# Moving the first transposed operands of a blocked triangular inversion ahead, and waiting group by group

## The reference

```
L = where(tri_strict, einsum('bhnid,bhnjd->bhnij', k_beta, kc) * decay, 0.0)
A = L + eye(C)
rhs = concatenate([vc * bc[..., None], k_beta * exp(gc)[..., None]], axis=-1)
sol = triangular_solve(A, rhs, left_side=True, lower=True, unit_diagonal=True)
u, w = sol[..., :Dv], sol[..., Dv:]
```

## Time and profile before

| | us |
|---|---|
| median of 3 runs | 2391.99 (2386.74 to 2392.05) |
| profiled execution, its own time | 2380.26 |
| its span | 2378.5 |
| TensorE busy | 2283.2 (96%) |
| VectorE busy | 1521.1 (64%) |
| ScalarE busy | 1071.8 (45%) |
| GpSimd busy | 540.3 (23%) |

### The profile page before, as it was taken

One profiled execution on the slowest core, in us unless ns is written; L12 is line 12 of the kernel. 1 busy time (PEld: TensorE's weight loads), 2 busy tenths in 40 slices (PEclk: granted clock), 3 DMA queues, 4 the chain that ended last, 5 costly groups with the idle time before them and its releaser, 6 DMA issues.

```text
span 2378.5 us, 41225 instructions
## 1 busy us (share of the span) xinstructions
PE 2283.2 (96%) x17949; PEld 2190.6 (92%) x17949; DVE 1521.1 (64%) x1826; ACT 1071.8 (45%) x1354; POOL 540.3 (23%) x276
## 2 busy tenths in 40 slices
PE   7998999999999989999999999998999999998999
PEld 7997988899989989898999999878999999878999
DVE  6854676677769256666766655686555655686554
ACT  2653356443345433654344434545344434546433
POOL 0923304499527232046500000000000000000000
PEclk8997999999999979999999999999999999999999
DMA  9751034667657300446655555423555555423553
GB/s 286 247 190 36 1 125 142 213 232 247 213 166 254 130 18 1 159 157 208 205 183 188 175 180 186 150 90 116 186 185 188 175 180 187 150 89 125 182 191 124
DMA packets 332862, 384.22 MB, mean 162 GB/s; under 512 B 12551, under 2 KB 315402, under 8 KB 332554
## 3 DMA queue, kind: packets, MB, share of 16 engines
q1 hardware_dynamic: 332234, 381.42, 49.0%
q10 hardware_dynamic: 448, 0.16, 0.0%
HBM read 380.51 MB, written 1.05 MB: 160 GB/s over the span
## 4 chain that ended last, share of the span: by engine, by line
PE 79%; DVE 11%; ACT 6%; issue 2%; DMA 0%; SPq 0%; ACTq 0%; DVEq 0%
PE bank L697 16%; PE bank L698 15%; PE bank L699 15%; PE bank L920 5%; PE bank L921 5%; PE bank L922 5%; DVE weights_low L1310 4%; ACT weights_high L1985 3%; PE bank L1115 2%; PE bank L1134 2%; PE bank L971 1%; DVE arena L1412 1%; PE bank L711 1%; PE bank L1093 1%; PE bank L983 1%
## 5 line engine op out<-in xcount | busy, mean ns | idle before, releaser
L1310 DVE TENSOR_TENSOR weights_low<-ring,weights_high 128x2048 fp32r<-128x2048 f32 x302 | 743.1, 2461 | 458.0 <-ACT weights_high L1985 457.9
L697 PE MATMUL bank<-h_high,weights_high 128*128 128x256 f32 x3296 | 943.5, 286 | 23.4 <-DVE weights_low L1310 14.2
L698 PE MATMUL bank<-h_low,weights_high 128*128 128x256 f32 x3296 | 928.4, 282 | 0.0
L699 PE MATMUL bank<-h_high,weights_low 128*128 128x256 f32 x3296 | 927.9, 282 | 0.0
L1985 ACT ACTIVATE weights_high<-ring 128x2048 fp32r<-128x2048 f32 x302 | 578.1, 1914 | 705.7 <-PE bank L699 521.6
L697 PEld LDWEIGHTS bank<-h_high,weights_high 128*128 128x128 f32 x3296 | 623.0, 189 | 40.5 <-DVE weights_low L1310 22.3
L698 PEld LDWEIGHTS bank<-h_low,weights_high 128*128 128x128 f32 x3296 | 623.9, 189 | 3.0 <-issue 2.9
L699 PEld LDWEIGHTS bank<-h_high,weights_low 128*128 128x128 f32 x3296 | 623.9, 189 | 0.0
L920 PE MATMUL bank<-hidden_high,weights_high 128*128 128x256 f32 x1056 | 300.3, 284 | 1.3 <-DVE hidden_low L1551 0.8
L921 PE MATMUL bank<-hidden_low,weights_high 128*128 128x256 f32 x1056 | 299.7, 284 | 0.0
L922 PE MATMUL bank<-hidden_high,weights_low 128*128 128x256 f32 x1056 | 299.5, 284 | 0.0
(11 more groups left out here) (409 smaller groups left out, 3101.8 us busy)
## 6 DMA issues: line engine op xcount, KB each, us to landing
ring<-in_w_in SPq DMA_DIRECT2D x80, 1024.0 KB, 5.1
ring<-in_w_up SPq DMA_DIRECT2D x44, 1024.0 KB, 5.3
ring<-in_ffn_w_gate SPq DMA_DIRECT2D x44, 1024.0 KB, 5.2
ring<-in_ffn_w_up SPq DMA_DIRECT2D x44, 1024.0 KB, 5.2
ring<-in_ffn_w_down SPq DMA_DIRECT2D x44, 1024.0 KB, 4.9
side<-in_w_ada SPq DMA_DIRECT2D x42, 1024.0 KB, 7.6
ring<-in_w_down SPq DMA_DIRECT2D x22, 1024.0 KB, 5.0
ring<-in_w_dn_out SPq DMA_DIRECT2D x8, 1024.0 KB, 5.1
```

The source lines that it names most:

```text
L697: mm(o[:, m, :], a_, high[:, t, :], start=(t == 0), stop=False)
L698: mm(o[:, m, :], a_, low[:, t, :], start=False, stop=False)
L699: last = mm(o[:, m, :], b_, high[:, t, :], start=False, stop=(t == KT - 1))
L1310: v.tensor_tensor(low, wide(q), high.bitcast(F32), ALU.subtract).then_inc(chunk_split, 1)
```

## The change

Level 0 is taken out of VectorE's loop over levels and written out by two helpers: `first_turned(g)` makes YT of a group and counts a new semaphore `yt_first`; `first_level(g)` makes Y and counts `y_updated`. YT of groups 0 and 1 is made inside the preparation, after `exponents(2)` and `rows(1)`; then come, after the preparation, YT 2, Y 0, Y 1, YT 3, Y 2, Y 3. Level 0's transposes wait for three groups' preparation instead of four, level 1's products of group g for g + 3 (at most 4) updates instead of four. GpSimd's level 1 mask waits for `yt_first` of its group, and TensorE's second product of level 1 too.

```diff
@@ -1101,9 +1102,9 @@
                         if s == 0 and g < 2:
-                            pe.wait_ge(d_rows, 4 * l + 4)
+                            pe.wait_ge(d_rows, 4 * l + 3)
                         if s == 1:
-                            pe.wait_ge(y_updated, 4 * (LEVELS * l + 1))
+                            pe.wait_ge(y_updated, 4 * LEVELS * l + min(g + 3, 4))
@@ -1126,6 +1127,8 @@
                         pe.wait_ge(w_copied, wn + 1)
+                        if s == 1:
+                            pe.wait_ge(yt_first, 4 * l + g + 1)
@@ -1688,11 +1691,28 @@
+                def first_turned(g):
+                    dve.wait_ge(offdiag_ready, 4 * LEVELS * l + g + 1)
+                    v.tensor_tensor(YT[:, g, :, :], over(ident, 4), LO[:, g, :, :], ALU.subtract).then_inc(yt_first, 1)
+
+                def first_level(g):
+                    dve.wait_ge(winv_done, 4 * LEVELS * l + g + 1)
+                    v.tensor_tensor(Y[:, g, :, :], over(ident, 4), f4(B[g % 2][:, :]), ALU.subtract).then_inc(y_updated, 1)
+
                 for g in range(5):
                     if g < 4:
                         exponents(g)
                     if g >= 1:
                         rows(g - 1)
+                    if g == 2:
+                        first_turned(0)
+                        first_turned(1)
+                first_turned(2)
+                first_level(0)
+                first_level(1)
+                first_turned(3)
+                first_level(2)
+                first_level(3)
@@ -1701,16 +1721,10 @@
-                for s in range(LEVELS):
+                for s in range(1, LEVELS):
                     for g in range(4):
-                        n = 4 * (LEVELS * l + s) + g
...
-                        if s == 0:
-                            dve.wait_ge(winv_done, n + 1)
-                            then(v.tensor_tensor(Y[:, g, :, :], over(ident, 4), f4(B[g % 2][:, :]), ALU.subtract))
-                            v.tensor_tensor(YT[:, g, :, :], over(ident, 4), LO[:, g, :, :], ALU.subtract).then_inc(y_updated, 1)
-                            continue
@@ -2403,7 +2417,7 @@
                         if s == 1:
-                            pool.wait_ge(y_updated, 4 * LEVELS * l + g + 1)
+                            pool.wait_ge(yt_first, 4 * l + g + 1)
```

More of the change, by code:

```diff
@@ L341, in build @@
         yinv_done = sem("yinv_done")
+        yt_first = sem("yt_first")
         yt_turned = sem("yt_turned")
```

## The result

| | us |
|---|---|
| before, median of 6 runs | 2389.36 (2377.1 to 2392.45) |
| changed, median of 6 runs | 2369.72 (2366.07 to 2371.55) |
| ratio | 0.993, 95% interval 0.9913 to 0.9948 |
| profiled execution after: its time, its span | 2371.4, 2369.6 |

The change gains 12 to 21 us by this measurement. Two later ones of the same kernel, with 30 and 17 runs of before beside it, say 0.9943 (0.9924 to 0.9962) and 0.9942 (0.9919 to 0.9964), so 13 to 14 us is the better figure. The forecast was 8.6 us, and 2369.7 lies outside its range.

The account below looks back on a forecast made before the run. TensorE, busy 96%, was taken to bound the kernel, idling in level 0 behind VectorE's Y and YT. A shift of 4.3 us in each of two layers, 8.6 us off 2391.99, gave 2383.4 us, range 2377 to 2390.

Parts of the forecast that it names:

- What bounds the place, and the order on VectorE: Level 0: VectorE's YT, stretched by GpSimd masks, delays level 1's first product; reordering shifts it 4.3 us earlier per layer.
- YT of groups 0 and 1 at no cost: Preparation: two YT of 0.69 us fit VectorE's 4.38 us idle time, ending 1.9 us ahead of need.
- The clash at 860.14: Level 0, second layer: YT of group 2 starts before GpSimd's mask of group 3 and passes in 0.69 us.
- rival 2: Level 0: GpSimd's mask goes ahead of YT of group 2; gain 3.5 us per layer, 2385.0 us; chance 0.15.
- The clock: Level 1: the rise to 2.4 GHz stays 4.8 us behind the first product, so it costs nothing new.
- the sum: Both layers' inversions: 2 × 4.3 = 8.6 us gained, with nothing counted for the clock.
- rival 3: Level 1: clock rises sooner because TensorE idles less; up to 2.3 us more per layer, 13.2 in all, 2378.8; chance 0.12.
- The margin of GpSimd: Level 1: masks of groups 1 to 3 end ahead of their products, by a margin of 1.3 us.
- The time: Whole kernel: 8.6 us off the three-run median of 2391.99 gives 2383.4 us.

Follow-up runs that it names:

- longer filling: Kernel before, with 3, 3 and 24 transposes of the identity put into TensorE's three idle places of level 0, no Y or YT moved; ratio 0.9984 (0.9967 to 1.0001).
- YT 0, 1 not hidden: Changed kernel with YT of groups 0 and 1 made right behind the preparation instead of in VectorE's idle time; ratio to kernel before 0.9980 (0.9967 to 0.9994).

## Why the prediction was wrong

- *What bounds the place, and the order on VectorE: right.* YT on the chain, stretched by GpSimd's masks, was the cause. The forecast shift was 4.3 us per layer, the trace has 4.4 to 4.5.
- *YT of groups 0 and 1 at no cost: right.* YT of group 1 in the second layer starts at 847.93 and ends 1.92 us before VectorE's next work, as forecast; what it saves was never priced apart in the forecast, and is about half of the gain (7.2 us).
- *The clash at 860.14: right.* VectorE passed, rival 2 did not come.
- *The clock: this is the step that failed.* "I take the rise to move with the work, which is what both layers show ... and the clock costs nothing new." The rise neither moves with the first product nor keeps its instant. Counted from L784 (L785), it came 15.2 to 15.4 us later in three of the four layers of before and 3.9 to 5.0 us later in all six layers of the changed kernel. That is 4.7 to 4.9 us behind the first product before, and 1.0 to 1.9 us ahead of it after. So the clock, which the sum put at nothing, gives 2.0 us per layer on top. The equal 4.8 us of the two layers that the forecast read are no rule: the second trace of the same kernel has 3.0 us in its first layer with the same idle time (2.86 us) in front, and the lowered counts alone have 5.7 and 6.4. The longer filling shows that less idle time among and behind the transposes is enough to have the clock up. Exactly which idle time in which layer loses it is not shown. The result is rival 3, with 13.2 us at a chance of 0.12; the inversions' 12.7 to 13.1 us are its number.
- *Why rival 3 was held for small.* Two arguments. "Four groups of transposes stood between 860.37 and 866.10 and the clock did not rise behind them": they stood there with 0.75, 0.88 and 2.83 us of idle time behind them, and the second trace of before shows it rising among them all the same, in one layer. And the Trainium skill (TensorE: Matmul & The Clock Gate, Part 4) says that transposes don't engage the full clock. The longer filling contradicts it for fp32 transposes of 128x128: the clock rose 2.7 us into a stretch of them, and stayed up through 2.78 us of them.
- *The margin of GpSimd: right only at the low clock.* The 1.3 us were counted with 1.71 us per group. At the full clock the groups follow each other in 0.95, and the last mask sets the fourth product; this holds back 0.1 us per layer. And 0.6 to 0.7 us stay idle before the first product where 0.2 to 0.4 were forecast, since the last transposes run at the full clock and end sooner.
- *The time.* The sum was carried to the median of three runs, 2391.99. Over three larger sets of its runs (30, 32 and 17) the median of before is 2385.09, 2386.88 and 2388.11. So the starting point was 4 to 7 us high, a miss of its own beside the clock's 4: 2385.09 less 12.8 is 2372.3, 2388.11 less 12.8 is 2375.3, against medians of 2369.7 to 2373.1 measured.

## What to carry to other kernels

Where TensorE stands idle just ahead of dense work at the low clock, a shorter idle time can pay twice: by the shift, and by the clock that is then up when the work begins. Price both. A distance from the work to the rise that two layers of one trace share is not yet a rule; look at a second trace, and at the idle places ahead of the work. And keep a VectorE instruction with two SBUF inputs out of the way of a GpSimd stream that it releases itself: hidden in an idle place it costs 0.69 us, behind a mask of the stream 1.3 to 1.8.

## What the runs showed of the hardware

- Transposes raise and hold the granted clock: in the longer filling it rose 2.7 us into a stretch of fp32 transposes behind L784 and stayed up through 24 more. At the full clock four take 0.63 us, at the low one 1.06 to 1.09.
- In level 0 the clock rose 3.3 to 5.2 us behind the start of L784 (L785) in all 16 layers with at most 0.4 us of idle time behind the first eight transposes. With 0.74 us or more it did so in two of six, and was lost again before level 1 in both. These are all layers but those of YT 0, 1 not hidden, where 2.75 us and more stood there.
- Idle time after a rise may lose the clock or not: with 1.95 us the products took 3.77 us in one layer and 5.27 in the other, with 1.99 us 5.27 and 5.28; 1.54 us lost it and 1.14 did not; with 0.58 to 0.74 us none of eight layers lost it. The 2.83 us of the kernel before don't tell: in three of its four layers the clock had not risen ahead of them, in the fourth it was already lost.
- Of a VectorE and a GpSimd instruction that both read SBUF, the one begun first passed in the clashes shown here: YT took 0.69 us when 0.16 us ahead of a mask, and 1.33 when behind one.
